# Two gate vectors summed as rows on four column groups and spread over the partitions through DRAM

## The chip, the cores and the metric

The kernel runs on one core of a Trainium2 chip. The metric is the time of the whole kernel on the device, in microseconds, the median of three runs. Beside it stands one profiled execution, whose trace is read below.

## What is computed

A trunk of two layers over 256 tokens of width 1024, all in f32. Layer 0 mixes tokens with gated linear attention (GLA), layer 1 with MoBA, a block-sparse softmax attention that has a single block of 256 keys here. Each mixer is followed by a squared-ReLU MLP of width 4096. Each of the four sub-layers is normalised and modulated (shift, scale) from a conditioning vector c, and its output is multiplied by a gate vector before it is added to x:

```python
c_act = jax.nn.silu(c)
for i in range(DEPTH):
    mod = (c_act @ ada_w[i] + ada_b[i])[:, None, :]
    sh1, sc1, g1, sh2, sc2, g2 = jnp.split(mod, 6, axis=-1)
    h = rms_norm(x, norm_mix_g[i]) * (1 + sc1) + sh1
    y = gla_mixer(h, ...) if i % 2 == 0 else moba_mixer(h, ...)
    x = x + g1 * y
    h = rms_norm(x, norm_mlp_g[i]) * (1 + sc2) + sh2
    x = x + g2 * sq_relu_mlp(h, mlp_w1[i], mlp_w2[i])
```

The four gates g1, g2 of the two layers are vectors of 1024 values. In the kernel tokens lie on the partitions, so a gate has to stand in every one of the 128 partitions.

## The kernel before

Every weight matrix goes through the same pipeline in pieces of 1 MB. SyncE's queue (SP) loads a piece into w_raw, ScalarE copies each half of it (a "unit" of 128 x 1024) to a rounded high part (L1051), and VectorE subtracts to get the low part (L1433). TensorE multiplies three times for each product, high by high, high by low and low by high (L503 to L505, L510 to L512, L698 to L700). The engines run programs written out by hand, in order, tied by counting semaphores; what stands ahead in an engine's program holds what is behind it.

The modulation c_act @ ada_w is computed beside the weights. GpSimd loads ada_w in pieces of 1 MB (load(s), L381), VectorE multiplies each by its values of c_act and accumulates over the rows that one partition has (ada(), L1450). What is left is a sum over the 128 partitions. For a shift or scale, sum_mods (L583) takes four blocks of 512 columns at once: each is multiplied by a 128 x 32 matrix of ones into its own 32 partitions of a PSUM bank. For a gate, fin_gate (L622) multiplies one block of 512 columns by 128 x 128 ones, so that the sum stands in all 128 partitions of a bank, and VectorE's gate() (L1486) adds it to the bias, which was loaded as a broadcast into the tile gates. A gate has two such blocks. The tile has room for two gates: slot 0 for a mixer's, slot 1 for an MLP's. Slots are filled again for layer 1 (gate_biases(1), L432), after SP has seen the last residual of layer 0.

The change touches these places in the order of time:
- Start: GpSimd's set-up memsets (L365, L366) ahead of its load of inv_f (L368); later, after load(5), the loads of the gate biases of layer 0 (L395).
- End of the first MLP, mlp(0) after the loop, from 326 us. TensorE: two fin_gate for the MLP's gate (blocks 10 and 11, L731), then sum_mods for the two sub-layers of layer 1. Then the last 48 products of the MLP, first the two halves of token tile 0, with the transposes of the modulation rows (L591) between them, then token tile 1. After three of the four units of tile 1 it waits for gate_ok and transposes the normalised tile 0 for MoBA (turn_norm, L631).
- VectorE there: the last split, gate() twice, two splits of MoBA's weights into the tile spare, then for each half of token tile 0 the residual, product with the gate (L1598) and addition to x (L1601), with mods() and one more split between the two. Then the norm of tile 0 (L1505 to L1509), and the low parts of its operands (L1587). ScalarE squares each half of x as it comes (L1073) and makes the operands (L1114, L1118).
- SP waits for x_new of token tile 1 of this residual, loads both gate biases of layer 1 (L432) and then goes on with MoBA's weights.
- MoBA. two_blocks runs the first two blocks of 512 columns of its input projection, and gate1() in it sums the gate of MoBA (blocks 16 and 17) after the second unit of the last group. VectorE's gate1() adds it to the bias, between two splits. turn_rot(0) (L906) transposes the first rotated tile (L1770) and waits for that gate, since both use banks 2 and 3. The gate is used by the residual at the end of MoBA.

Of the kernel before, what the change touches and what calls it, by code (L numbers as in the profile page):

```python
# [25 lines left out]
F32 = mybir.dt.float32  # L26
# [21 lines left out]
def trunk_kernel(nc, x_d, c_d, pos_d, ada_w, ada_b, mix_g, mlp_g, gla_in, gla_up, gla_bg, gla_og,  # L48
# [32 lines left out]
    with ctx:  # L81
# [17 lines left out]
        gates = sb("gates", [P, 2, D])  # L99
        eye = sb("eye", [P, P])  # L100
# [111 lines left out]
        gb_in = [sem(f"gb_in{i}") for i in range(DEPTH)]  # L212
        hi_made, lo_made = sem("hi_made"), sem("lo_made")
# [138 lines left out]
        def _(pool):  # L352
# [14 lines left out]
            pool.wait_ge(pool_set, 2)  # L367
# [6 lines left out]
            for k in range(4):  # L374
                nc.gpsimd.dma_start(glr_up[32 * k:32 * k + RANK, :], gla_up[0]).then_inc(glr_in, 16)
            def load(s):
# [12 lines left out]
            for s in range(2, 4 * N_PAIRS_ADA):  # L389
                pool.wait_ge(ada_mac, 2 * (s - 1))  # L390
                load(s)
                if s == 5:
                    nc.gpsimd.dma_start(amask[:, :], amask_d).then_inc(mask_in, 16)
                    for i in range(2):
                        nc.gpsimd.dma_start(gates[:, i], ada_b[0:1, (3 * i + 2) * D:(3 * i + 3) * D].to_broadcast([P, D])  # L395
                                            ).then_inc(gb_in[0], 16)
# [3 lines left out]
        def _(sp):  # L400
# [28 lines left out]
            def gate_biases(l):  # L429

                for s in range(2):
                    sp.dma_start(gates[:, s], ada_b[l:l + 1, (3 * s + 2) * D:(3 * s + 3) * D].to_broadcast([P, D])  # L432
                                 ).then_inc(gb_in[l], 16)
# [65 lines left out]
        def _(pe):  # L499
# [123 lines left out]

            def turn_norm(v, tb):
# [52 lines left out]
            def mlp(l):  # L677
# [52 lines left out]
                for i in range(2):  # L730
                    fin_gate(12 * l + 10 + i, i)  # L731
                if l + 1 < DEPTH:
# [18 lines left out]
                for u in range(4 if l + 1 < DEPTH else 0):  # L751
# [3 lines left out]
                    if u == 2:  # L755
                        pe.wait_ge(gate_ok, 4 * l + 4)
# [134 lines left out]
            def moba():  # L891
                def gate1():
                    pe.wait_ge(a_ok, A_NORM[2] + 8)
                    for i in range(2):
                        fin_gate(16 + i, 2 + i)

                def turn_rot(n):

                    pe.wait_ge(rot_ok, n + 1)
                    if n == 0:  # L900
                        pe.wait_ge(gate_ok, 6)
# [56 lines left out]
                two_blocks(2, mix_base[1], [in_bank(n, tb) for n in range(2) for tb in range(TB)], {1: gate1})  # L958
# [452 lines left out]
        def _(dve):  # L1411
# [69 lines left out]
            def gate(i, bank):  # L1481

                dve.wait_ge(gb_in[i // 4], 32)
                dve.wait_ge(gate_p, i + 1)
                g = gates[:, (i % 4) // 2, (i % 2) * COLS:(i % 2 + 1) * COLS]
                V.tensor_tensor(g, ps[:, bank, :], g, ALU.add).then_inc(gate_ok, 1)  # L1486

# [242 lines left out]
            def moba():  # L1730
# [43 lines left out]
                def gate1():  # L1774
                    for i in range(2):
# [240 lines left out]
```

## Time and profile before

| | us |
|---|---|
| median of 3 runs | 643.25 |
| lowest and highest | 642.64 to 643.25 |
| span of the profiled execution | 642.6 |
| TensorE busy | 617.6 |
| VectorE busy | 474.3 |
| ScalarE busy | 341.8 |
| GpSimd busy | 39.5 |

All times below are microseconds from the start of the profiled span, unless ns is written. Busy times of an engine leave out its waits and the issuing of DMAs. A line of a timeline gives start, length, engine, line of the kernel, what is written and read, and in brackets how long the engine stood idle before it and what released it. The chain is followed back from the last instruction, at each step to what released it. A time to landing runs from the issue of a DMA to its last byte and semaphore.

### The profile page before, as it was taken

What the parts mean: (1) busy time and instruction counts of PE and PEld (TensorE: products, weight loads), DVE (VectorE), ACT (ScalarE), POOL (GpSimd) and SP (SyncE); (2) the same over time, 40 slices, a digit from 0 to 9 for tenths busy, and PEclk for the clock granted to TensorE, in tenths of its full rate; (3) what the DMA queues carried; (4) which work ended last, traced back from release to release, by engine and by line L of the source; (5) the groups of instructions that cost most, each with busy time, mean ns of one, the idle gap of its engine ahead of it and who ended that gap; (6) DMA issues with size and microseconds to landing.
All of it is one profiled execution on the core that took longest, in us unless ns stands there. A gap on an engine that the chain in (4) does not pass through costs nothing.

```text
span 642.6 us, 9093 instructions
## 1 busy us (share of the span) xinstructions
PE 617.6 (96%) x3391; PEld 515.0 (80%) x3391; DVE 474.3 (74%) x660; ACT 341.8 (53%) x581; POOL 39.5 (6%) x65
## 2 busy tenths in 40 slices
PE   3699999999999999999999999999999999999997
PEld 2367875677889989998977788788789899899985
DVE  4638998898778978889897898766786555455455
ACT  3437632658654354445458688666954453444440
POOL 3030011000000101010100000000000000000000
PEclk9699999999999999999999999999999999999999
DMA  8999599678488998999982665344476555556501
GB/s 287 387 356 395 180 318 384 224 247 277 156 284 316 376 366 306 351 363 337 360 320 82 246 197 196 133 126 155 132 267 225 171 182 188 191 196 196 196 0 65
DMA packets 59084, 156.43 MB, mean 243 GB/s; under 512 B 2818, under 2 KB 3312, under 8 KB 59056
## 3 DMA queue, kind: packets, MB, share of 16 engines
q1 hardware_dynamic: 47296, 112.41, 49.9%
q0 software_dynamic: 11760, 43.67, 19.2%
q8 instruction: 15, 0.25, 0.2%
q14 instruction: 13, 0.11, 0.0%
HBM read 155.02 MB, written 1.05 MB: 243 GB/s over the span
## 4 chain that ended last, share of the span: by engine, by line
PE 82%; DVE 10%; DMA 3%; issue 2%; ACT 2%; SPq 0%; DVEq 0%; ACTq 0%
PE ps L503 14%; PE ps L504 14%; PE ps L505 14%; PE ps L700 7%; PE ps L699 7%; PE ps L698 7%; PE ps L510 4%; PE ps L511 3%; PE ps L512 3%; DMA arena<-in_ada_w_dram 3%; DVE w_lo L1433 1%; DVE spare L1433 1%; DVE ada_acc L1450 1%; PE ps L607 1%; PE ps L622 1%
## 5 line engine op out<-in xcount | busy, mean ns | idle before, releaser
L1051 ACT ACTIVATE w_hi<-w_raw 128x1024 fp32r<-128x1024 f32 x180 | 189.2, 1058 | 205.0 <-PE ps L505 107.0
L1433 DVE TENSOR_TENSOR w_lo<-w_raw,w_hi 128x1024 fp32r<-128x1024 f32 x180 | 217.9, 1222 | 94.5 <-ACT w_hi L1051 94.3
L699 PE MATMUL ps<-a_lo,w_hi 128*128 128x256 f32 x384 | 108.7, 283 | 0.0
L700 PE MATMUL ps<-a_hi,w_lo 128*128 128x256 f32 x384 | 108.7, 283 | 0.0
L698 PE MATMUL ps<-a_hi,w_hi 128*128 128x256 f32 x384 | 108.6, 283 | 0.0
L503 PE MATMUL ps<-w_hi,m_hi 128*128 128x512 f32 x256 | 100.4, 392 | 0.0
L504 PE MATMUL ps<-w_lo,m_hi 128*128 128x512 f32 x256 | 99.8, 390 | 0.0
L505 PE MATMUL ps<-w_hi,m_lo 128*128 128x512 f32 x256 | 99.7, 389 | 0.0
L503 PE MATMUL ps<-w_hi,a_hi 128*128 128x512 f32 x224 | 92.7, 414 | 5.1 <-DVE a_lo L1587 5.1
L504 PE MATMUL ps<-w_lo,a_hi 128*128 128x512 f32 x224 | 88.3, 394 | 0.0
L505 PE MATMUL ps<-w_hi,a_lo 128*128 128x512 f32 x224 | 88.3, 394 | 0.0
L1450 DVE SCALAR_TENSOR_TENSOR ada_acc<-ada_raw,c_act,ada_acc 128x1024 f32<-128x1024 f32 x56 | 71.8, 1281 | 3.6 <-DMA ada_raw<-in_ada_w_dram 2.0
L698 PEld LDWEIGHTS ps<-a_hi,w_hi 128*128 128x128 f32 x384 | 73.7, 192 | 0.5
L699 PEld LDWEIGHTS ps<-a_lo,w_hi 128*128 128x128 f32 x384 | 73.7, 192 | 0.5
L700 PEld LDWEIGHTS ps<-a_hi,w_lo 128*128 128x128 f32 x384 | 73.7, 192 | 0.0
L503 PEld LDWEIGHTS ps<-w_hi,a_hi 128*128 128x128 f32 x224 | 42.6, 190 | 19.2 <-issue 7.4
L503 PEld LDWEIGHTS ps<-w_hi,m_hi 128*128 128x128 f32 x256 | 48.1, 188 | 11.3 <-DVE w_lo L1433 0.8
L505 PEld LDWEIGHTS ps<-w_hi,m_lo 128*128 128x128 f32 x256 | 48.1, 188 | 10.1
L504 PEld LDWEIGHTS ps<-w_lo,m_hi 128*128 128x128 f32 x256 | 48.1, 188 | 9.4
L381 POOL DMA_DIRECT2D ada_raw<-in_ada_w_dram x40 | 28.2, 706 | 406.4 <-DVE ada_acc L1450 361.3
L505 PEld LDWEIGHTS ps<-w_hi,a_lo 128*128 128x128 f32 x224 | 42.6, 190 | 9.3
L504 PEld LDWEIGHTS ps<-w_lo,a_hi 128*128 128x128 f32 x224 | 42.7, 191 | 8.0
(202 smaller groups left out, 708.9 us busy)
## 6 DMA issues: line engine op xcount, KB each, us to landing
w_raw<-in_mlp_w_dram SPq DMA_DIRECT2D x64, 1024.0 KB, 5.5
ada_raw<-in_ada_w_dram POOLq DMA_DIRECT2D x40, 1024.0 KB, 6.7
w_raw<-in_gla_w_in_dram SPq DMA_DIRECT2D x12, 1024.0 KB, 14.7
w_raw<-in_moba_w_in_dram SPq DMA_DIRECT2D x12, 1024.0 KB, 7.3
ada_raw<-in_ada_w_dram SPq DMA_DIRECT2D x4, 1024.0 KB, 13.2
arena<-in_ada_w_dram SPq DMA_DIRECT2D x4, 1024.0 KB, 14.3
w_raw<-in_gla_w_out_dram SPq DMA_DIRECT2D x4, 1024.0 KB, 9.3
w_raw<-in_moba_w_out_dram SPq DMA_DIRECT2D x4, 1024.0 KB, 5.0
```

Source lines behind the costliest of these rows:

```text
L381: nc.gpsimd.dma_start(ada_pair(s), src.rearrange("(k p) n -> p k n", p=P)).then_inc(ada_sw_in[s % 2], 16)
L503: mm(out, hi, w_hi[:, slot, wc], start=first, stop=False)
L504: mm(out, hi, w_lo[:, slot, wc], start=False, stop=False)
L505: return mm(out, lo, w_hi[:, slot, wc], start=False, stop=last)
L510: mm(out, hi, unit_hi(u)[:, wc], start=first, stop=False)
L511: mm(out, hi, unit_lo(u)[:, wc], start=False, stop=False)
L698: mm(o, w_hi[:, u, w], a_hi[:, a, :], start=u == 0 and k == 0, stop=False)
L699: mm(o, w_hi[:, u, w], a_lo[:, a, :], start=False, stop=False)
L700: z = mm(o, w_lo[:, u, w], a_hi[:, a, :], start=False, stop=u == 3 and k == 1)
L1051: A(dst, w_raw[:, c // 2, c % 2], ACT.Copy).then_inc(hi_made, 1)
L1433: V.tensor_tensor(out, w_raw[:, c // 2, c % 2], w.bitcast(F32), ALU.subtract).then_inc(lo_made, 1)
L1450: z = V.scalar_tensor_tensor(acc, w, c, acc, op0=ALU.mult, op1=ALU.add)
```

## The change

The gate of the first MLP (blocks 10, 11) and that of MoBA (blocks 16, 17) are summed together at the end of the first MLP. Four products with 128 x 32 ones put them as rows into partitions 0, 32, 64 and 96 (and their neighbours) of one bank. VectorE adds the biases, which GpSimd loaded into four rows of a new tile gate_row, in one instruction. GpSimd, once it has issued load(37), waits for that, stores the four rows to a DRAM tensor of 2 x 1024, waits until they are all there, and loads each gate from it as a broadcast into its slot of gates, the MLP's first. VectorE waits for the MLP's broadcast before the first residual of the seam, and for the other before the residual of MoBA. Both fin_gate and both gate() inside MoBA are gone, as are those of the first MLP; the first gate (GLA's) and the last (the second MLP's) stay as they were. SP loads only one bias for layer 1. TensorE's waits for the old gates become a wait for gate_row_ok at the seam and for the operands in MoBA.

```diff
+        gate_row = sb("gate_row", [97, COLS])
+        gate_d = nc.dram_tensor("gate_rows", [2, D], F32).ap()
...
-            pool.wait_ge(pool_set, 2)
+            nc.gpsimd.memset(gate_row[:, :], 0.0).then_inc(pool_set, 1)
+            pool.wait_ge(pool_set, 3)
...
+            def bias_row(at, l, part):
+
+                for i in range(2):
+                    c0 = part * D + i * COLS
+                    nc.gpsimd.dma_start(gate_row[32 * (at + i):32 * (at + i) + 1, :], ada_b[l:l + 1, c0:c0 + COLS]
+                                        ).then_inc(bias_row_in, 16)
...
-                    for i in range(2):
-                        nc.gpsimd.dma_start(gates[:, i], ada_b[0:1, (3 * i + 2) * D:(3 * i + 3) * D].to_broadcast([P, D])
-                                            ).then_inc(gb_in[0], 16)
+                    nc.gpsimd.dma_start(gates[:, 0], ada_b[0:1, 2 * D:3 * D].to_broadcast([P, D])).then_inc(gb_in[0], 16)
+                    bias_row(0, 0, 5)
+                    bias_row(2, 1, 2)
+                if s == 37:
+                    pool.wait_ge(gate_row_ok, 1)
+                    for j in range(4):
+                        nc.gpsimd.dma_start(gate_d[j // 2:j // 2 + 1, (j % 2) * COLS:(j % 2 + 1) * COLS],
+                                            gate_row[32 * j:32 * j + 1, :]).then_inc(row_out, 16)
+                    pool.wait_ge(row_out, 64)
+                    for r in range(2):
+                        nc.gpsimd.dma_start(gates[:, 1 - r], gate_d[r:r + 1, :].to_broadcast([P, D])
+                                            ).then_inc(gate_in[1 - r], 16)
...
-                for s in range(2):
-                    sp.dma_start(gates[:, s], ada_b[l:l + 1, (3 * s + 2) * D:(3 * s + 3) * D].to_broadcast([P, D])
-                                 ).then_inc(gb_in[l], 16)
+                sp.dma_start(gates[:, 1], ada_b[l:l + 1, 5 * D:6 * D].to_broadcast([P, D])).then_inc(gb_in[l], 16)
...
+            def sum_gates(blocks, bank):
+
+                pe.wait_ge(ada_mac, 8 * (ada_turn(blocks[-1]) + 1))
+                for i, b in enumerate(blocks):
+                    z = mm(ps[32 * i:32 * i + 32, bank, :], ones[:, 0:32], ada_acc[:, acc_slot(b)],
+                           start=True, stop=True)
+                z.then_inc(row_p, 1)
...
-                for i in range(2):
-                    fin_gate(12 * l + 10 + i, i)
-                if l + 1 < DEPTH:
+                if l + 1 == DEPTH:
+                    for i in range(2):
+                        fin_gate(22 + i, i)
+                else:
+                    sum_gates((10, 11, 16, 17), 0)
...
-                        pe.wait_ge(gate_ok, 4 * l + 4)
+                        pe.wait_ge(gate_row_ok, 1)
...
-                        pe.wait_ge(gate_ok, 6)
+                        pe.wait_ge(a_ok, A_NORM[2] + 8)
...
+            def gate_rows(bank):
+
+                dve.wait_ge(bias_row_in, 64)
+                dve.wait_ge(row_p, 1)
+                V.tensor_tensor(gate_row[:, :], ps[0:97, bank, :], gate_row[:, :], ALU.add).then_inc(gate_row_ok, 1)
...
                 spare_units(3, range(2))
+                dve.wait_ge(gate_in[0], 16)
...
-                for i in range(2):
-                    gate(4 * l + 2 + i, i)
                 if l + 1 < DEPTH:
+                    gate_rows(0)
                     spare_units(2, range(2))
-                dve.wait_ge(gate_ok, 4 * l + 4)
+                    dve.wait_ge(gate_in[1], 16)
+                else:
+                    for i in range(2):
+                        gate(2 + i, i)
+                    dve.wait_ge(gate_ok, 4)
```

## Rows read from the trace of the kernel before

**Rows 1.** The page: busy times; the chain that ended last.

```profile
PE 617.6 (96%) x3391; PEld 515.0 (80%) x3391; DVE 474.3 (74%) x660; ACT 341.8 (53%) x581; POOL 39.5 (6%) x65
...
PE 82%; DVE 10%; DMA 3%; issue 2%; ACT 2%; SPq 0%; DVEq 0%; ACTq 0%
```

**Rows 2.** Chain in order of time, gate and modulation sums: start, length, what.

```profile
326.67 1.72 PE ps L622 x4
328.38 1.90 PE ps L583 x16
...
362.27 1.72 PE ps L622 x4
```

**Rows 3.** Timeline, TensorE, seam: start, length, instruction, [idle before, releaser].

```profile
341.51 1.06 PE L631 MATMUL ps<-eye,arena 128*128 128x128 f32 x8 [0.62 <-DVE arena L1509]
```

**Rows 4.** Timeline of VectorE, end of the first MLP and entry into MoBA.

```profile
321.06 2.60 DVE L1450 SCALAR_TENSOR_TENSOR arena<-ada_raw,c_act,arena 128x1024 f32<-128x1024 f32 x2
...
329.99 1.29 DVE L1486 TENSOR_TENSOR gates<-ps,gates 128x512 f32<-128x512 f32 x2
...
334.16 0.69 DVE L1598 TENSOR_TENSOR arena<-ps,gates 128x512 f32<-128x512 f32 x1
...
340.56 0.81 DVE L1509 TENSOR_SCALAR arena<-x,stat 128x1024 f32<-128x1024 f32 x1
```

**Rows 5.** Timeline of VectorE in MoBA's first two blocks.

```profile
366.57 1.28 DVE L1486 TENSOR_TENSOR gates<-ps,gates 128x512 f32<-128x512 f32 x2
...
369.92 1.23 DVE L1770 TENSOR_TENSOR arena<-arena,stat 128x1024 f32<-128x1024 f32 x1
```

**Rows 6.** Timeline of TensorE in MoBA: the first rotated transposes.

```profile
372.04 1.03 PE L906 MATMUL ps<-eye,arena 128*128 128x128 f32 x8
```

**Rows 7.** Timeline of GpSimd.

```profile
3.48 1.95 POOL L354 DMA_DIRECT2D rows<-in_ada_b_dram  x4
...
5.67 0.55 POOL L366 MEMSET glr_up<- 128x512 f32 x1
...
88.90 0.71 POOL L381 DMA_DIRECT2D ada_raw<-in_ada_w_dram  x1 [3.16 <-DVE ada_acc L1450]
...
323.96 0.70 POOL L381 DMA_DIRECT2D ada_raw<-in_ada_w_dram  x1 [4.08 <-DVE arena L1450]
```

**Rows 8.** DMA issues: out, in, queue, count, KB, us to landing.

```profile
x<-in_x_dram SPq DMA_DIRECT2D x2, 512.0 KB, 4.1
gates<-in_ada_b_dram POOLq DMA_DIRECT2D x2, 512.0 KB, 9.5
gates<-in_ada_b_dram SPq DMA_DIRECT2D x2, 512.0 KB, 4.7
out_dram<-x SPq DMA_DIRECT2D x4, 256.0 KB, 2.0
...
glr_up<-in_gla_w_gate_up_dram POOLq DMA_DIRECT2D x4, 32.0 KB, 6.1
...
pos_i<-in_positions_dram POOLq DMA_DIRECT2D x1, 1.0 KB, 2.0
```

**Rows 9.** Windows: length, busy of each engine (instructions), PEclk, DMA share, GB/s.

```profile
330.20:334.16 3.96, 3.96 (x26) 3.37 (x23) 3.35 (x4) 3.85 (x5) 0.00 (x0) 1.00 1.01 391
334.16:341.50 7.34, 6.73 (x30) 5.25 (x29) 5.85 (x15) 4.28 (x10) 0.00 (x0) 1.00 0.21 79
```

**Rows 10.** Windows of the start-up, same columns.

```profile
16.00:20.00 4.00, 2.57 (x21) 1.36 (x17) 3.07 (x10) 0.60 (x1) 0.00 (x0) 0.95 1.05 388
...
24.00:28.00 4.00, 1.08 (x6) 0.99 (x5) 2.81 (x6) 2.72 (x5) 0.00 (x0) 0.50 1.04 387
```

**Rows 11.** The chain in the start-up: start, length, what.

```profile
32.57 0.43 PE ps L503
...
33.39 0.23 PE ps L505
```

**Rows 12.** Timeline of VectorE in the start-up.

```profile
25.12 0.16 DVE L1459 TENSOR_TENSOR modc<-ps,cols 128x4 f32<-128x4 f32 x1 [4.84 <-PE ps L615]
```

More of the change, by code:

```diff
@@ L212, in trunk_kernel @@
         gb_in = [sem(f"gb_in{i}") for i in range(DEPTH)]
+        bias_row_in, row_p, gate_row_ok, row_out = sem("bias_row_in"), sem("row_p"), sem("gate_row_ok"), sem("row_out")
+        gate_in = [sem(f"gate_in{i}") for i in range(2)]
         hi_made, lo_made = sem("hi_made"), sem("lo_made")
@@ L891, in moba @@
             def moba():
-                def gate1():
-                    pe.wait_ge(a_ok, A_NORM[2] + 8)
-                    for i in range(2):
-                        fin_gate(16 + i, 2 + i)
                 def turn_rot(n):
@@ L957, in moba @@
                 pe.wait_ge(x_new, x_done(2, 0, 1))
-                two_blocks(2, mix_base[1], [in_bank(n, tb) for n in range(2) for tb in range(TB)], {1: gate1})
+                two_blocks(2, mix_base[1], [in_bank(n, tb) for n in range(2) for tb in range(TB)], {})
                 for n in range(2, 6):
@@ L1481, in gate @@
             def gate(i, bank):
-                dve.wait_ge(gb_in[i // 4], 32)
+                dve.wait_ge(gb_in[i // 2], 16)
                 dve.wait_ge(gate_p, i + 1)
-                g = gates[:, (i % 4) // 2, (i % 2) * COLS:(i % 2 + 1) * COLS]
+                g = gates[:, i // 2, (i % 2) * COLS:(i % 2 + 1) * COLS]
                 V.tensor_tensor(g, ps[:, bank, :], g, ALU.add).then_inc(gate_ok, 1)
+            def gate_rows(bank):
+                dve.wait_ge(bias_row_in, 64)
+                dve.wait_ge(row_p, 1)
+                V.tensor_tensor(gate_row[:, :], ps[0:97, bank, :], gate_row[:, :], ALU.add).then_inc(gate_row_ok, 1)
             def newton(r, v, b, r0):
@@ L1772, in scale @@
                                     r[:, :, None].to_broadcast([P, 8, HD]), ALU.mult).then_inc(rot_ok, 1)
-                def gate1():
-                    for i in range(2):
-                        gate(4 + i, 2 + i)
                 def top(h):
@@ L1805, in follow @@
                         rotate(0)
-                    if (n, u) == (1, 0):
-                        gate1()
                     if 1 <= n < 4:
@@ L1898, in mlp @@
                         hidden(NJ - 1, base + 8 * NJ - 4)
-                for i in range(2):
-                    gate(4 * l + 2 + i, i)
                 if l + 1 < DEPTH:
+                    gate_rows(0)
                     spare_units(2, range(2))
-                dve.wait_ge(gate_ok, 4 * l + 4)
+                    dve.wait_ge(gate_in[1], 16)
[3 more added lines that the diff above has]
+                    dve.wait_ge(gate_ok, 4)
                 for half in range(2):
```

## Prediction

> **What bounds the kernel now.** I read the page's busy shares and its chain first. TensorE is busy 96% of the span, and the chain that ended last is 82% TensorE [rows 1]. So TensorE work taken away is worth its full time wherever TensorE doesn't stop to wait, and every new stop is lost in full. The change touches two places of that engine's queue: the end of the first MLP with the entry into the MoBA layer (I call it the seam, 326 to 350 us), and the inside of MoBA's first two projection blocks (362 us). I then read the timelines of TensorE and VectorE over both, because there one wait has to be followed from engine to engine.
>
> At the seam TensorE runs two full gate sums from 326.67, 1.72 us on the chain, then two modulation sums of eight matmuls each [rows 2]. It goes straight on with the last 48 products of the MLP and stops only once, for 0.62 us until 341.51: the transposes of the next norm wait for VectorE's normalised tile (L1509) [rows 3, 4]. VectorE's queue to that tile is: gate additions at 329.99, two splits of weights, first residual at 334.16, then the modulation vectors, a split and the second residual, norm at 340.56 [rows 4]. From residual to the end of the norm that is 341.37 - 334.16 = 7.2 us. VectorE doesn't wait for TensorE anywhere in it, so this queue of VectorE, with ScalarE's squares in between, sets when TensorE goes on. Cover at the seam is therefore short: a first residual that comes later by d makes TensorE late by the whole of d, because the stop exists already.
>
> **What the change takes away.** At the end of the first MLP two full sums (1.72 us on the chain) become one group of four column-group sums. A modulation sum has that form, 16 steps of them take 1.90 us on the chain, thus 0.95 us for a group [rows 2]. TensorE saves 1.72 - 0.95 = 0.8 us there, but that only makes it arrive earlier at the stop at 341.51. I cost it at nothing; if the new wait below did not exist it would still be worth at most nothing to 0.6 us, since VectorE's queue is what is late. VectorE saves one addition of 0.64 us, hidden in the same way by the new wait.
>
> In MoBA both full gate sums go, 1.72 us on the chain [rows 2], in a stretch where TensorE never stops. The 1.28 us of additions on VectorE go too [rows 5]. What could be late next there is VectorE's rotated tile L1770, done at 369.92 + 1.23 = 371.15, for the transposes at 372.04 [rows 5, 6]. TensorE would come to them at 370.3; VectorE, 1.28 us lighter, is ready at 369.9. So the full 1.7 us is gained, and I see no wait that takes it back. Bounds: 1.3 us if VectorE's lightening is all that passes, 1.8 us at most.
>
> **What it adds: a round trip.** The summed rows must be added to the biases, stored to DRAM by GpSimd, waited for, and read back as two broadcasts; the first residual of the seam now waits for the broadcast of the MLP gate. Step by step:
> - The addition stands where the old ones stood, behind the last weight split on VectorE. It starts at 329.99 and takes half of the pair's 1.29 us, to 330.65 [rows 4]. That TensorE delivers earlier doesn't help.
> - GpSimd sees a semaphore of VectorE 0.30 us after the instruction's end (multiply-adds 321.06 + 2.60 = 323.66, load at 323.96 [rows 4, 7]). At 323.96 it issued the last weight load before this point and then it only waits, so nothing is in front. First store at 330.95.
> - Four stores are issued in a row. A small one costs the queue 1.95 / 4 = 0.49 us [rows 7]; the fourth starts at 330.95 + 3 x 0.49 = 332.4.
> - Landing of a store of 2 KB from GpSimd to DRAM isn't in the trace. The nearest rows: the 1 KB load by GpSimd and the stores of the output, both 2.0 us, before and after the full load of the DMA; 32 KB loads by GpSimd at a time of full DMA 6.1 [rows 8]. Here the DMA engines are full (share 1.01) until 334 and then empty out (mean share 0.21 to 341.5) [rows 9]. I take 4.0, the middle of 2.0 and 6.1: 336.4. It could be no lower than 2.0, as that is the floor of every row.
> - GpSimd wakes, 0.30: 336.7. The broadcast of 512 KB: 4.7 us by SP's queue for a pair, 4.1 for a plain 512 KB load, 9.5 by GpSimd's queue at a full time [rows 8]. The engines are empty by then, so I take 4.7: 341.4.
> - First residual at 341.45 instead of 334.16: 7.3 us late. All of VectorE's and ScalarE's queue behind it (both residuals, modulation vectors, norm, the operands of MoBA's first block) is late by as much, and TensorE with it. TensorE reaches its stop 0.8 us earlier, at 340.1, and would stand until 348.8: about 8.7 us. Two other queues stand behind this: SP's wait for x_new holds MoBA's next weight loads, late by as much and no more, and behind GpSimd's new waits are only the last two modulation loads, which the second MLP asks for over 100 us later.
>
> As to a rule for these two transfers: the Trainium skill (DMA: Bandwidth & Descriptors, Anatomy of one DMA) gives a GpSimd transfer 2.0 us plus bytes / 436e3 us. By it the store takes 2.0 and the broadcast 3.2 us, an estimate by that page, and the residual would start at 337.9, 3.8 us late; the sum would be 645.3 without and 647.6 with the clock term below. The trace's own 512 KB row of 4.1 us is already above the page's 3.2.
>
> **The clock after the stop.** In the start-up TensorE worked 2.57 of the 4 us from 16 to 20 and the mean granted clock was 0.95 there: it fell just before 20. From 24 to 28, with 1.08 us of work, it was 0.50 (1.2 GHz instead of 2.4) [rows 10]. The dense work that began at 28.39 ran at 0.43 us a product until 33.0, after which it was 0.23 [rows 11]. That is 11 products with 0.20 us extra each, 2.2 us. A stop of 8.7 us is longer than all idleness in either of those two stretches, so I take it that the clock falls here and costs 2.2 us. Bounds: 0 and 2.5.
>
> The Trainium skill (TensorE: Matmul & The Clock Gate, Part 1) states that an idle array goes to 1.2 GHz and needs sustained work to get back. By that rule the fall here is certain; the rows show only the fall after half-idle work.
>
> **Other edits.** The memset of the row tile (as L366's, 0.55 us) moves GpSimd's load of inv_f by as much, and VectorE's angles with it. But VectorE later waits 4.84 us for TensorE's columns, up to 25.12 [rows 12], which covers 0.55; uncovered it would cost 0.55. Four small bias loads replace one broadcast by GpSimd near 85 us: four issues of 0.49 are 2.0 us, less the one removed, in front of an idle of 3.16 us [rows 7]. SP issues one gate load less behind its wait for x_new, so the weight loads after it can only come sooner. All three at nothing.
>
> **Sum.** Profiled span 642.6; the median 643.25 is 0.65 above it, and I add the differences to the median. +7.3 (late residual) + 2.2 (clock) - 1.7 (MoBA's gate sums) = +7.8: 651.0 us.
>
> **Rivals.**
> - *The clock doesn't fall.* For it: it was at 1.00 for nearly all of 16 to 20 us with TensorE idle a third of the time [rows 10]. +7.3 - 1.7 = +5.6: 648.8. With the short landings (2.0 and 4.1) the residual starts at 338.8, 4.7 late, and the time is 646.2.
> - *The transfers are slow.* For it: the trace's two broadcasts by GpSimd's queue took 9.5 us [rows 8], and this is that form. Landings 6.1 and 9.5 put the residual at 348.3, 14.1 late: +14.6 with the clock: 657.9. Against it: those rows come from a time of full DMA.
> - *The round trip is covered, and the kernel is faster.* VectorE still has two splits to do before the residual, so the trip has from 330.65 to 334.16 for nothing, and breaks even with MoBA's gain up to 335.9. If it is all covered the time is 643.25 - 1.7 = 641.5. It needs both transfers and five issues in 5.2 us; the floor rows (2.0 and 4.1, with issues of 1.5 and wakes of 0.6) already add to 8.2. Only if the time to landing of these forms is far under any row can it be.
> - *The change doesn't do what it says:* the four sums run one after another instead of side by side. Then the seam loses nothing either, as TensorE is early at the stop; the time stays at 651.0.
>
> **How the numbers follow.** Forecast (clock falls, landings between 2.0 + 4.1 and 6.1 + 4.7): 0.58, 648.4 to 653.1. Clock stays: 0.22, 646.2 to 650.9. Slow transfers: 0.12, to 657.9. Covered: 0.05. Something between covered and the shortest landings: 0.03. Range 646.2 to 655.5: it leaves out the covered cases and the upper half of the slow one, some 0.15. This kernel's times can be told apart to about 0.2% (1.3 us): faster 0.05, same 0.02, slower 0.93.
>
> **What would show it.** VectorE idle before the first residual of the seam, released by the broadcast, some 8 us. TensorE idle before L631's transposes at about 341 us grown from 0.62 to 6 to 10 us. Granted clock 0.5 for some us behind it, with products of 0.43. No gate sum between 345 and 372 us (shifted), and the distance from MoBA's first product to its first rotated transposes shorter by 1.7 us. The forecast falls if the broadcast lands before 336, or if TensorE's stop is as short as now.

## The result and the profile after

The changed kernel takes 650.38 us (median of 4, 649.97 to 651.26) against 642.94 us before; the ratio is 1.0112, 95% interval 1.0096 to 1.0128. It is slower by 7.4 us, where 7.8 had been forecast.

| | before | after |
|---|---|---|
| median, us | 642.94 | 650.38 |
| span of the profiled execution | 642.6 | 648.4 |
| TensorE busy | 617.6 | 615.4 |
| VectorE busy | 474.3 | 472.4 |
| GpSimd busy | 39.5 | 44.8 |

The page of after, its busy times and its chain, beside [rows 1]:

```profile
PE 615.4 (95%) x3391; PEld 514.4 (79%) x3391; DVE 472.4 (73%) x657; ACT 341.6 (53%) x581; POOL 44.8 (7%) x75
...
PE 77%; DVE 12%; DMA 5%; issue 3%; ACT 2%; SPq 0%; POOL 0%; DVEq 0%; ACTq 0%
```

TensorE is busy 2.2 us less and the kernel is longer: the shares of VectorE, the DMA and issue in the chain have grown, that of TensorE has shrunk. The timeline of VectorE at the seam, which answers to [rows 4]:

```profile
328.00 0.68 DVE L1516 TENSOR_TENSOR gate_row<-ps,gate_row 97x512 f32<-97x512 f32 x1
328.82 2.36 DVE L1457 TENSOR_TENSOR spare<-w_raw,spare 128x1024 fp32r<-128x1024 f32 x2
340.20 0.69 DVE L1628 TENSOR_TENSOR arena<-ps,gates 128x512 f32<-128x512 f32 x1 [9.02 <-DMA gates<-gate_rows]
...
346.58 0.81 DVE L1539 TENSOR_SCALAR arena<-x,stat 128x1024 f32<-128x1024 f32 x1
```

Then GpSimd over the same time, and TensorE at the four sums, the transposes, the first product of MoBA and the first rotated transposes (beside [rows 3] and [rows 6]):

```profile
328.98 1.97 POOL L412 DMA_DIRECT2D gate_rows<-gate_row  x4 [6.32 <-DVE gate_row L1516]
336.13 1.07 POOL L416 DMA_DIRECT2D gates<-gate_rows  x2 [5.18 <-DMA gate_rows<-gate_row]
```

```profile
324.39 1.06 PE L647 MATMUL ps<-ada_acc,ones 128*32 128x512 f32 x8
...
347.54 1.94 PE L658 MATMUL ps<-eye,arena 128*128 128x128 f32 x8 [9.70 <-DVE arena L1539]
...
351.52 0.39 PE L529 MATMUL ps<-spare,a_hi 128*128 128x512 f32 x1
...
377.77 1.03 PE L930 MATMUL ps<-eye,arena 128*128 128x128 f32 x8
```

**How to compare the two traces.** The seam comes 2.0 us earlier in the profiled execution of after (addition at 328.00 against 329.99), before anything of the change but its start-up edits has happened. Those edits change nothing that the times show (experiment 2), so I put the 2.0 us down to scatter of single executions and take distances from that addition. In microseconds:
- addition to first residual: 4.17 before, 12.20 after: 8.0 late;
- first residual to the transposes: 341.51 - 334.16 = 7.35 before, 347.54 - 340.20 = 7.34 after: nothing is made up;
- transposes to MoBA's first product: 344.10 - 341.51 = 2.59 before, 351.52 - 347.54 = 3.98 after: 1.4 more;
- MoBA's first product to the rotated transposes: 372.04 - 344.10 = 27.94 before, 377.77 - 351.52 = 26.25 after: 1.7 less.

The sum is 8.0 + 1.4 - 1.7 = +7.7. From the addition to the end of the span it is 642.6 - 329.99 = 312.6 before and 648.4 - 328.00 = 320.4 after, +7.8: nothing else happens behind the seam.

The windows of TensorE's clock in after, of 1 us each (length, busy time of PE, PEld, DVE, ACT, POOL, then PEclk, DMA share, GB/s):

```profile
340.00:341.00 1.00, 0.00 (x0) 0.00 (x0) 0.77 (x2) 0.00 (x0) 0.00 (x0) 0.95 0.64 262
341.00:342.00 1.00, 0.00 (x0) 0.00 (x0) 0.95 (x4) 0.35 (x1) 0.00 (x0) 0.50 0.00 0
...
350.00:351.00 1.00, 1.00 (x4) 0.71 (x4) 0.42 (x1) 0.97 (x3) 0.00 (x0) 0.50 0.00 0
351.00:352.00 1.00, 1.00 (x6) 0.82 (x5) 0.27 (x1) 0.97 (x4) 0.00 (x0) 0.93 0.00 0
```

TensorE's products end at 337.8; the granted clock falls to 0.50 (1.2 GHz) just before 341 and is back just after 351.0, 3.5 us after the transposes began. It was low for ten microseconds, but for six and a half of them TensorE had nothing to do. How much of the low stretch falls on work differs between executions, as the table behind experiment 8 shows.

### The profile page after: what moved, and what is told of

The parts are those of the page before. It is cut to its first block, busy times and chain, and to the rows that moved or that the text cites. A ratio compares the mean times of both kernels' runs of the same rounds, so it can differ in the third digit from the quotient of the medians.

```text
span 648.4 us, 9096 instructions
## 1 busy us (share of the span) xinstructions
PE 615.4 (95%) x3391; PEld 514.4 (79%) x3391; DVE 472.4 (73%) x657; ACT 341.6 (53%) x581; POOL 44.8 (7%) x75
## 3 DMA queue, kind: packets, MB, share of 16 engines
HBM read 155.02 MB, written 1.06 MB: 241 GB/s over the span
## 4 chain that ended last, share of the span: by engine, by line
PE 77%; DVE 12%; DMA 5%; issue 3%; ACT 2%; SPq 0%; POOL 0%; DVEq 0%; ACTq 0%
PE ps L522 13%; PE ps L523 13%; PE ps L524 13%; PE ps L727 7%; PE ps L726 7%; PE ps L725 7%; PE ps L529 4%; PE ps L531 3%; PE ps L530 3%; DMA arena<-in_ada_w_dram 2%; DVE w_lo L1457 2%; DMA ada_raw<-in_ada_w_dram 2%; DVE spare L1457 1%; DVE arena L1474 1%; DVE ada_acc L1474 1%
## 6 DMA issues: line engine op xcount, KB each, us to landing
ada_raw<-in_ada_w_dram SPq DMA_DIRECT2D x4, 1024.0 KB, 12.9
```

## Experiments

**1. Nobody waits for the trip.** The stores and broadcasts stay, but slot 1 of the gates is filled early with the biases alone. So this kernel leaves out the summed part of the first MLP's gate and its output is not the reference's.

```diff
+                    nc.gpsimd.dma_start(gates[:, 1], ada_b[0:1, 5 * D:6 * D].to_broadcast([P, D])).then_inc(gate_in[1], 16)
                     bias_row(0, 0, 5)
...
-                    for r in range(2):
-                        nc.gpsimd.dma_start(gates[:, 1 - r], gate_d[r:r + 1, :].to_broadcast([P, D])
-                                            ).then_inc(gate_in[1 - r], 16)
+                    nc.gpsimd.dma_start(gates[:, 0], gate_d[0:1, :].to_broadcast([P, D])).then_inc(cut_in, 16)
+                    pool.wait_ge(cut_in, 16)
+                    nc.gpsimd.dma_start(gates[:, 0], gate_d[1:2, :].to_broadcast([P, D])).then_inc(gate_in[0], 16)
```

> The changed kernel with the round trip left in place but nobody waiting for it: the broadcast of the first MLP's gate row goes to slot 0 and is overwritten by MoBA's, and slot 1 holds the biases alone, loaded at 85 us. So the first MLP's output is multiplied by its gate's bias and not by the whole gate. Theory A (the loss is VectorE's wait for the broadcast, 8.0 us, and 1.4 us of slow TensorE clock behind it; MoBA's two gate sums give 1.7 us back): 641.2 us, TensorE's stop at the seam back at under 1 us, clock 1.00 there. Rival B (the stores, the broadcasts and GpSimd's issues cost by themselves, by contention or as time outside the span): 645 or more.

Measured: 640.88 us against 643.16 before, ratio 0.9957 (0.9937 to 0.9977). VectorE at the seam, then TensorE at the transposes:

```profile
327.66 0.68 DVE L1518 TENSOR_TENSOR gate_row<-ps,gate_row 97x512 f32<-97x512 f32 x1
328.89 2.36 DVE L1459 TENSOR_TENSOR spare<-w_raw,spare 128x1024 fp32r<-128x1024 f32 x2 [0.55 <-ACT spare L1077]
331.17 0.68 DVE L1630 TENSOR_TENSOR arena<-ps,gates 128x512 f32<-128x512 f32 x1
```

```profile
338.51 1.06 PE L660 MATMUL ps<-eye,arena 128*128 128x128 f32 x8 [0.59 <-DVE arena L1541]
```

With the same sums, stores and GpSimd work, the whole loss is gone once the wait is gone. Rival B is refuted. The gain is 2.3 us by the medians (1.5 to 4.1 by the interval), where MoBA's sums account for 1.7. In the traces the other 0.6 lies at the seam: from the addition to the residual it is 3.51 us here and 4.17 before (4.37 in experiment 2, which has the old sums too). The split on VectorE waits for ScalarE's copy (0.55 in the row above; 0.60 before), ScalarE's copies stand behind its reading of the modulation rows, and these behind TensorE's sums. So most of TensorE's saving gets through to VectorE, where nothing else holds it; that VectorE itself has one addition less is needed for it too.

**2. The start-up edits alone**, on the kernel before: tile, memset, and the four loads of bias rows.

```diff
+            nc.gpsimd.memset(gate_row[:, :], 0.0).then_inc(pool_set, 1)
+            pool.wait_ge(pool_set, 3)
...
+                            nc.gpsimd.dma_start(gate_row[32 * (at + i):32 * (at + i) + 1, :], ada_b[l:l + 1, c0:c0 + COLS]
+                                                ).then_inc(bias_row_in, 16)
```

> The kernel before with the start-up edits alone: the row tile, its memset, and four loads of bias rows (used by nobody), both broadcasts kept. In the trace of the changed kernel everything from the first matmuls of the start-up on is about 2 us earlier than before, while the time outside its span is about 1.2 us longer. Theory A: neither belongs to the change; 642.9 us within 0.6. Rival B: the edits move the start-up by 1 to 2 us either way, 641 or 644.5.

Measured: 643.05 against 643.16 us, ratio 0.9996 (0.9983 to 1.0009). Nothing clear of the noise, as theory A has it. The first weight product of the start-up, first in after, then in this kernel:

```profile
27.49 0.77 PE L522 MATMUL ps<-w_hi,a_hi 128*128 128x512 f32 x1 [3.30 <-DVE a_lo L1617]
```

```profile
25.38 0.76 PE L511 MATMUL ps<-w_hi,a_hi 128*128 128x512 f32 x1 [3.31 <-DVE a_lo L1595]
```

It stood at 28.39 before, 3.0 us later than in this kernel with an equal median. Among traces with this same start-up code it stands between 25.38 and 28.08 (experiment 4). It doesn't carry over to the seam as it is: the gate additions come at 328.89 here against 329.99 before, 1.1 us apart and not 3.0. So neither number says much about a change. The times of the kernel before, measured beside experiments 5 to 8, lie between 642.15 and 645.61, and in each of those executions the time is 1.7 us or more above the span. So the profiled execution of before, with its span of 642.6, was one of the slower of its kind.

**3. TensorE kept busy in its stop** with 36 spare products.

```diff
+                        for _ in range(WARM):
+                            mm(ps[:, 0, :], m_hi[:, 3, tile(1)], w_hi[:, 3, 0:COLS], start=True, stop=True)
                         pe.wait_ge(mod_red, 4 + v + 2)
                         turn_norm(v + 1, 0)
```

> The changed kernel with 36 spare products of 128 x 512 (each 0.23 us, 8.3 us in all) put into the 9.7 us in which TensorE stands before the next norm's transposes. Their result is not used. Theory A (the granted clock falls in the stop and costs 1.4 us after it): the clock stays 1.00, transposes take 1.06 us instead of 1.94, time 649.0. Rival B (the slow clock is covered by ScalarE and VectorE, which are what is late): clock 1.00 but time 650.4 as without.

Measured: 649.39 us, ratio 1.0101 (1.0077 to 1.0125): 6.2 us above before, against 7.4. TensorE, then two windows:

```profile
338.46 8.32 PE L788 MATMUL ps<-w_hi,m_hi 128*128 128x512 f32 x36
347.84 1.06 PE L659 MATMUL ps<-eye,arena 128*128 128x128 f32 x8 [1.05 <-DVE arena L1542]
...
350.43 0.47 PE L530 MATMUL ps<-spare,a_hi 128*128 128x512 f32 x1
```

```profile
346.00:348.00 2.00, 0.95 (x6) 0.52 (x5) 1.49 (x4) 1.97 (x4) 0.00 (x0) 1.00 0.00 0
348.00:350.00 2.00, 2.00 (x14) 1.68 (x13) 0.97 (x2) 1.62 (x5) 0.00 (x0) 1.00 0.00 0
```

The clock stays at 1.00 and transposes to MoBA's first product takes 350.43 - 347.84 = 2.59 us, to the hundredth what it took before. The clock's part is 1.4 us in this pair of traces. The times give 0.7 (by the ratios) to 1.2, with an interval (1.0077 to 1.0125) that overlaps that of after, so they alone show no gain. The table behind experiment 8 has more traces for it.

**4. The row sum earlier.** The same sum behind the first unit of down projection j = 5, with the last two turns of TensorE's loop written out, VectorE's addition after its multiply-adds of unit c = 4, the stores behind modulation load 33 and the broadcasts behind load 34.

```diff
-                with pe.Fori(1, NJ - 1) as j:
+                with pe.Fori(1, NJ - 3 if l == 0 else NJ - 1) as j:
...
+                    def rows_now():
+                        pe.wait_ge(relu_ok, 2 * (m0 + NJ - 2) + 2)
+                        sum_gates((10, 11, 16, 17), 0)
...
+                        if l == 0 and c == 4 and isinstance(j, int) and j == NJ - 3:
+                            gate_rows(0)
```

> The changed kernel with the same four-row sum one and a half blocks of the MLP earlier, behind the first unit of the down projection j = 5 (about 296 us), and the trip behind modulation loads 33 and 34. Nothing waits for it at the seam. Theory A: the residual starts when VectorE comes to it; the seam has 1.72 us less on TensorE, 0.9 us of row sums are paid in the loop, MoBA gives 1.7 us: 640.4 us, faster than both. Rival B (the trip is slow because the DMA is full, and it slows the weights that the loop needs, or the early sum makes TensorE wait for VectorE): 642 or more.

Measured: 643.13 us, ratio 0.9995 (0.9983 to 1.0007). The seam's wait is gone and so is the gain. GpSimd, then VectorE:

```profile
308.96 1.06 POOL L417 DMA_DIRECT2D gates<-gate_rows  x2 [1.38 <-DMA gate_rows<-gate_row]
310.48 0.71 POOL L393 DMA_DIRECT2D ada_raw<-in_ada_w_dram  x1 [0.47 <-DVE arena L1485]
```

```profile
323.48 2.60 DVE L1485 SCALAR_TENSOR_TENSOR arena<-ada_raw,c_act,arena 128x1024 f32<-128x1024 f32 x2 [3.79 <-DMA ada_raw<-in_ada_w_dram]
```

The multiply-adds at 323.48 need load 35, issued at 310.48 behind 1 MB of broadcasts in the same queue. It landed 12.9 us later; the median of these loads is 6.5 to 7.6 us, by the trace. Theory A missed what the broadcasts are in front of.

**5. The same with the broadcasts out of the way**: the MLP's behind load 35, MoBA's behind load 37.

```diff
-                if s == 34:
+                if s == 35:
                     pool.wait_ge(row_out, 64)
-                    for r in range(2):
-                        nc.gpsimd.dma_start(gates[:, 1 - r], gate_d[r:r + 1, :].to_broadcast([P, D])
-                                            ).then_inc(gate_in[1 - r], 16)
+                    nc.gpsimd.dma_start(gates[:, 1], gate_d[0:1, :].to_broadcast([P, D])).then_inc(gate_in[1], 16)
+                if s == 37:
+                    nc.gpsimd.dma_start(gates[:, 0], gate_d[1:2, :].to_broadcast([P, D])).then_inc(gate_in[0], 16)
```

> As e_early, but the broadcast of the MLP's gate is issued behind modulation load 35 instead of in front of it, and MoBA's behind load 37 at the seam. In e_early VectorE stood 3.79 us at 319.7 us for load 35, which was behind 1 MB of broadcasts in GpSimd's queue and took 12.9 us to land. Theory A (that stall was the whole of what was missing): it goes, and the time is 643.1 - 3.8 + 1.2 for what of it the seam would have absorbed, 640.5 us, or 0.9963 of before. Rival B (the early row sum costs the loop its time by itself, through VectorE being 97% busy there): 642 to 643.

Measured: 640.29 us against 643.20 before, ratio 0.9949 (0.9929 to 0.9968). It beats both kernels. GpSimd, VectorE and TensorE:

```profile
309.05 0.71 POOL L393 DMA_DIRECT2D ada_raw<-in_ada_w_dram  x1 [2.92 <-DVE arena L1485]
309.76 0.55 POOL L416 DMA_DIRECT2D gates<-gate_rows  x1
```

```profile
331.68 0.68 DVE L1639 TENSOR_TENSOR arena<-ps,gates 128x512 f32<-128x512 f32 x1
```

```profile
339.01 1.06 PE L659 MATMUL ps<-eye,arena 128*128 128x128 f32 x8 [0.57 <-DVE arena L1550]
```

The first residual waits for nothing. Rival B is refuted: what was missing in experiment 4 was the stall of 3.79 us, of which the times get back 2.8. That the row sums cost the loop no more than the seam is as far as the times tell: experiment 1, with the sums at the seam, has 0.9957 (0.9937 to 0.9977).

**6. The trip again at a quiet time**, by the same queue, behind the first.

```diff
+                    pool.wait_ge(gate_in[0], 16)
+                    pool.wait_ge(gate_in[1], 16)
+                    for j in range(4):
+                        nc.gpsimd.dma_start(gate_e[j // 2:j // 2 + 1, (j % 2) * COLS:(j % 2 + 1) * COLS],
+                                            gate_row[32 * j:32 * j + 1, :]).then_inc(row_out, 16)
+                    pool.wait_ge(row_out, 128)
+                    nc.gpsimd.dma_start(gates[:, 0], gate_e[1:2, :].to_broadcast([P, D])
+                                        ).then_inc(gate_in[0], 16)
```

> The changed kernel with a second trip right behind the first, by the same queue, from 341 us on, when the DMA engines are empty: four stores to another DRAM tensor and one broadcast of 512 KB of MoBA's gate. Theory A (full engines make the store slow): the second stores land in 2.0 to 2.5 us against 5.0 for the first, the broadcast in about 4 us as in the first trip. Rival C (GpSimd's way or the DRAM target makes it slow): 5 us again. The time is that of the changed kernel, 650.4, as nobody waits for the second trip.

Measured: 650.8 us in its one run. The DMA issues of this kernel (out, in, queue, count, KB, median us to landing):

```profile
gates<-gate_rows POOLq DMA_DIRECT2D x2, 512.0 KB, 4.6
...
gates<-gate_rows_again POOLq DMA_DIRECT2D x1, 512.0 KB, 3.7
...
gate_rows_again<-gate_row POOLq DMA_DIRECT2D x4, 2.0 KB, 1.5
```

and the chain of the same kernel over the first trip:

```profile
330.49 5.40 DMA gate_rows<-gate_row
```

The same store by the same queue takes 1.5 us when the DMA engines are idle and 5.4, from the last issue, when SP's weight loads are under way. So neither GpSimd's queue nor the DRAM target makes it slow by itself, and rival C is refuted in that form. The trip pays the difference, 3.9 us, for coming behind SP's loads.

What the store waits for can be read from the packets. The DMA of after from 332.5 to 335.5, SP's queue (q1) and GpSimd's (q0): packets, MB, share.

```profile
q1 hardware_dynamic: 294, 0.57, 49.1%
q0 software_dynamic: 128, 0.01, 2.9%
```

The four rows are 128 small packets here (the second trip above has 128 too). None of the rows' packets is sent before 332.5, 2 us after the last issue, and the last 4 of them go between 335.0 and 335.5 together with the last 2 of SP's. GpSimd goes on at 336.13. It is the same in every trace of a trip at the seam by this queue (last issue before the wait; the half microsecond with the last packets of SP's queue; GpSimd's next issue):

| trace | last issue | SP's last packets | GpSimd goes on |
|---|---|---|---|
| after | 330.46 | 335.0 to 335.5 | 336.13 |
| changed kernel, second trace | 330.35 | 334.5 to 335.0 | 335.40 |
| experiment 1 | 330.1 | 333.5 to 334.0 | 334.90 |
| experiment 3 | 330.84 | 335.0 to 335.5 | 336.31 |
| experiment 6 | 330.49 | 335.0 to 335.5 | 336.17 |
| experiment 8, first trace | 331.91 | 336.5 to 337.0 | 337.63 |
| experiment 8, second trace | 329.61 | 334.5 to 335.0 | 335.47 |

GpSimd goes on 0.4 to 0.9 us after SP's last half microsecond, and 4.8 to 5.9 us after the last issue. So in all seven the landing goes with the end of SP's loads and not with the issue; the time from issue to landing is what is left between the two. Why the last row packets go no earlier, with a DMA share of only 0.26 from 334.0, 0.06 from 334.5 and 0.02 from 335.0 in after, isn't shown.

**7. The trip by ScalarE's queue.** ScalarE issues the stores, does its four copies, waits for the stores and issues the broadcasts.

```diff
+                    act.wait_ge(gate_row_ok, 1)
+                    for j in range(4):
+                        nc.scalar.dma_start(gate_d[j // 2:j // 2 + 1, (j % 2) * COLS:(j % 2 + 1) * COLS],
+                                            gate_row[32 * j:32 * j + 1, :]).then_inc(row_out, 16)
                     spare_units(2)
+                    act.wait_ge(row_out, 64)
+                    for r in range(2):
+                        nc.scalar.dma_start(gates[:, 1 - r], gate_d[r:r + 1, :].to_broadcast([P, D])
+                                            ).then_inc(gate_in[1 - r], 16)
```

> The changed kernel with the four stores and two broadcasts issued by ScalarE's queue instead of GpSimd's: ScalarE waits for the row, issues the stores, copies four units of MoBA's weights (3.9 us), waits for the stores and issues the broadcasts. Theory A (the 5 us of a store are DMA engines full with SP's weights, whoever issues): about the same landings, the trip within 1 us of the 12.2 us of the changed kernel, time 649.5 to 651. Rival C (they belong to GpSimd's way of issuing): landings of 2 us as for the output's stores, the trip 3 us shorter, time 647.

Measured: 648.73 us, ratio 1.0088 (1.0062 to 1.0113). ScalarE, then VectorE (whose addition stands at 327.06 here):

```profile
327.78 1.35 ACTq L1408 DMA_DIRECT2D gate_rows<-gate_row  x4
329.23 3.90 ACT L1066 ACTIVATE spare<-w_raw 128x1024 fp32r<-128x1024 f32 x4 [1.91 <-issue]
333.08 0.83 ACTq L1413 DMA_DIRECT2D gates<-gate_rows  x2
```

```profile
337.03 0.69 DVE L1627 TENSOR_TENSOR arena<-ps,gates 128x512 f32<-128x512 f32 x1 [4.34 <-DMA gates<-gate_rows]
```

The trip is 337.03 - 327.06 = 10.0 us, 2.2 shorter than the 12.2 of after: more than theory A allowed and less than rival C asked. The first store goes out at once and not 0.30 us later and four issues take 1.35 instead of 1.97, together 0.6 us up to the last issue. The other 1.5 us lie between the last store's issue and the broadcast's: ScalarE comes back at 333.08, 4.2 us after its last issue at 328.9, and the rows have landed. The broadcast is 0.1 shorter. The packets show that the rows were there before ScalarE came. First from 330.5 to 333.0, then from 334.0 to 334.5 (q10 is ScalarE's queue; its later packets are the broadcasts'):

```profile
q1 hardware_dynamic: 333, 0.65, 71.9%
q10 hardware_dynamic: 8, 0.01, 0.9%
...
q10 hardware_dynamic: 21, 0.09, 68.1%
q1 hardware_dynamic: 3, 0.00, 2.2%
```

The four rows are 8 packets in this queue and not 128. All have gone by 332.5 (none is left between 332.5 and 334.0), 3.6 us after the last issue, while SP's queue still has packets behind 334.0. So theory A fails in "whoever issues": beside SP's loads the stores of this queue didn't wait for the drain in this trace, where GpSimd's did in all seven. That the number of packets is the reason isn't shown. By the times the gain of 1.7 us is likely but not beyond doubt: the intervals of this kernel and of after overlap (1.0113 and 1.0096), and this trace is of an execution of 646.78 us, 2.0 under the kernel's median.

**8. Two stores instead of four before the wait.**

```diff
-                    for j in range(4):
...
-                    pool.wait_ge(row_out, 64)
                     for r in range(2):
+                        for i in range(2):
+                            j = 2 * r + i
+                            nc.gpsimd.dma_start(gate_d[r:r + 1, i * COLS:(i + 1) * COLS],
+                                                gate_row[32 * j:32 * j + 1, :]).then_inc(row_out, 16)
+                        pool.wait_ge(row_out, 32 * (r + 1))
```

> The changed kernel with only the MLP gate's two rows stored before the wait; its broadcast goes out, then MoBA's two rows and broadcast follow. Theory A (a store lands a fixed time, 5 us, after its issue, so two issues of 0.49 us fewer shorten the trip by 1.0 us, and each us of the trip is a us of the kernel): 649.4 us, VectorE's wait 8.0 instead of 9.0. Rival B (stores land only when SP's weight loads have drained at about 335 us, however early they are issued): 650.3.

Measured: 651.50 us, ratio 1.0128 (1.0101 to 1.0154), although the trip in its trace was 1.1 us shorter (330.42 to 341.48). So it was measured once more, beside the changed kernel itself.

> The changed kernel as it is, once more, as the measure for the next one on the same chip: 1.0112 of before, 650.4 us. In its second profile the trip from the row's addition to the first residual should again take 12.2 us; executions differ by 1 to 2 us in the start-up and in the loads of the first MLP, ahead of the seam, so the distance from the row's addition to the end of the span is the better measure: 320.4 us again.

> The kernel of e_pair once more, since its time (651.5) and its trace disagreed: the trip had become 1.1 us shorter (11.1 against 12.2), but the seam came 2.4 us later in that execution, 1.9 of it from the first MLP's loads, where this kernel has no edit. Theory A (the trip's 1.1 us are gained, the rest was scatter ahead of the seam): 1.0 us under e_after of the same call, and 319.4 to 319.7 us from the row's addition to the end. Rival D (something of the edit costs it back behind the seam, MoBA's later stores and broadcast): the same time as e_after or more, and a distance of 320.4 or more.

Measured: the changed kernel 651.26 us, ratio 1.0116 (1.0093 to 1.0140); two stores first 649.97 us, ratio 1.0093 (1.0074 to 1.0111). GpSimd and VectorE of the changed kernel in its second trace:

```profile
328.87 1.96 POOL L412 DMA_DIRECT2D gate_rows<-gate_row  x4 [6.37 <-DVE gate_row L1516]
335.40 1.06 POOL L416 DMA_DIRECT2D gates<-gate_rows  x2 [4.57 <-DMA gate_rows<-gate_row]
```

```profile
339.60 0.69 DVE L1628 TENSOR_TENSOR arena<-ps,gates 128x512 f32<-128x512 f32 x1 [8.12 <-DMA gates<-gate_rows]
```

and of the kernel with two stores first:

```profile
329.10 1.02 POOL L414 DMA_DIRECT2D gate_rows<-gate_row  x2 [6.50 <-DVE gate_row L1517]
335.47 0.54 POOL L417 DMA_DIRECT2D gates<-gate_rows  x1 [5.36 <-DMA gate_rows<-gate_row]
```

```profile
339.44 0.69 DVE L1629 TENSOR_TENSOR arena<-ps,gates 128x512 f32<-128x512 f32 x1 [7.73 <-DMA gates<-gate_rows]
```

The trip was 12.2 and 11.7 us with four stores, 11.1 and 11.3 with two. But the saved issues are not the reason. The last row store was issued earlier (329.61 against 330.35 in the second traces) and its landing came no earlier: GpSimd goes on at 335.47 and 335.40, both times when SP's queue has drained (table in experiment 6). So for the store the rival B of the first expectation holds (stores land when SP's weight loads have drained), and theory A's fixed time after the issue is refuted: it is 5.4 and 5.6 us with two stores against 4.8 and 5.4 with four. What is shorter is the broadcast, which now goes out alone: from its issue to the residual 3.85 and 3.97 us against 4.07 and 4.20. The rest of the differences in the trip is when the loads drain: over the seven traces GpSimd goes on 7.2 to 8.2 us after the addition.

The times don't resolve any of this. The ratios were 1.0128 against 1.0112 of after at first, and 1.0093 against 1.0116 for the second pair, with intervals that overlap both times. From the addition to the end of the span, where 319.4 to 319.7 had been expected, it is 319.7 in the first trace and 648.5 - 328.1 = 320.4 in the second, against 648.4 - 327.9 = 320.5 for the changed kernel's second. Where the second trace loses what its shorter trip gained is seen in the table below: its low clock cost more.

**All traces side by side** (row sum added, first residual, span, and from the residual to the end of the span):

| trace | addition | residual | span | residual to end | clock at the transposes |
|---|---|---|---|---|---|
| before | 329.99 | 334.16 | 642.6 | 308.4 | 1.00 |
| experiment 1 | 327.66 | 331.17 | 637.9 | 306.7 | 1.00 |
| experiment 3 | 328.38 | 340.50 | 647.2 | 306.7 | 1.00 |
| experiment 4 | in the loop | 334.83 | 641.5 | 306.7 | 1.00 |
| experiment 5 | in the loop | 331.68 | 638.4 | 306.7 | 1.00 |
| after | 328.00 | 340.20 | 648.4 | 308.2 | 0.50 |
| changed kernel, second trace | 327.89 | 339.60 | 648.4 | 308.8 | 0.50 |
| experiment 6 | 328.02 | 340.46 | 649.0 | 308.5 | 0.50 |
| experiment 7 | 327.06 | 337.03 | 645.0 | 308.0 | 0.50 |
| experiment 8, first trace | 330.42 | 341.48 | 650.1 | 308.6 | 0.50 |
| experiment 8, second trace | 328.12 | 339.44 | 648.5 | 309.1 | 0.50 |

Wherever the clock stays, the kernels with the new sums have 306.7 us behind the residual, 1.7 less than before: that is MoBA's part. Wherever it falls they have 308.0 to 309.1, so the low clock costs 1.3 to 2.4 us, and the 1.4 to 1.5 of after is near the low end.

## Why the prediction was right, point by point

The mechanism held at each step. That the sum came within 0.4 us is in part luck: against the trace of after, the lateness was forecast 0.7 too short and the clock 0.8 too dear, and within the lateness the store was 1.4 too short and the broadcast 0.7 too long.

- **The late residual: 7.3 forecast, 8.0 measured.** The mechanism held step by step: the addition in its old place, a wake of GpSimd of 0.30 us, issues of 0.49, the wait, the broadcast. The store was mis-sized: 4.0 was taken, the middle between quiet and full, and it took 5.4 from the last issue. The 2.0 that the prediction called the floor of every row was not one either: a quiet store took 1.5. The prediction looked for a landing time, where the rows wait for SP's loads to drain (experiment 6). The trace before had that moment, but rows 9 hide it in a mean share of 0.21 up to 341.5. In before, in half microseconds (DMA share next to last):

```profile
336.50:337.00 0.50, 0.50 (x4) 0.42 (x3) 0.50 (x1) 0.16 (x1) 0.00 (x0) 1.00 0.09 33
337.00:337.50 0.50, 0.50 (x4) 0.42 (x3) 0.50 (x2) 0.00 (x0) 0.00 (x0) 1.00 0.00 0
```

SP's loads are over about 337.0 there, 7.0 us behind the addition. With them as the bound GpSimd would go on at 337.4 or later and not at 336.7. The broadcast, at a quiet time, took 4.0 where 4.7 was taken. In the other traces of kernels with this wait and GpSimd's four stores the residual is 7.5 to 8.3 us late, not always 8.0.
- **The Trainium skill's figure for the store.** The 2.0 us that the Trainium skill gives as the fixed cost of a GpSimd transfer (DMA: Bandwidth & Descriptors, Anatomy of one DMA) is close to the 1.5 us of the quiet store. Here it was 5.4 behind SP's loads, which the sentence doesn't cover. The Trainium skill (DMA: Bandwidth & Descriptors, Latency and other measured facts) has the memory's own latency grow tenfold at high load, from 0.2 to 2 us. That can't be what is long here: the rows' last packets go after 335.0, 4.5 us after the last issue, and GpSimd goes on 1.1 us later at most.
- **TensorE's wait equals VectorE's lateness.** Right: the stretch from residual to transposes is 7.35 and 7.34 us. The stop itself was forecast at 8.7 and was 9.7, since the trip was longer.
- **The clock: 2.2 forecast, 1.4 measured in after, 1.3 to 2.4 over six traces.** It fell, as forecast, and the start-up's rows had the right kind of event. In after the low clock lasted 3.5 us after work resumed and not the 4.6 of the start-up (28.39 to 33.0), and the first part of it is the eight transposes, 1.94 us instead of 1.06, behind which TensorE used to wait 0.15 us for VectorE anyway. The other traces show that this length differs from execution to execution, so 2.2 lies inside what single executions show. Experiment 3 confirms the term in its trace. The rival in which the clock stays is refuted for this stop: it fell in all six traces in which TensorE stood for 7.1 to 9.7 us.
- **MoBA's gate sums: 1.7 forecast, 1.7 measured** (27.94 to 26.25 us).
- **TensorE's earlier arrival at the seam**, costed at nothing: it was worth nothing in the changed kernel, where the new wait swallows it. But the reason given, that VectorE's queue alone is late, was incomplete: without the wait 0.66 us come through, by way of ScalarE (traces of experiment 1), just above the bound of 0.6.
- **The other edits at nothing:** right for those of the start-up, to within the interval of experiment 2. SP's one load less was not taken apart.
- **The rival "one after another"** is refuted: the four sums start at 324.39 and what follows at 325.27, so they take 0.88 us, where 0.95 was taken for a group side by side.
- **The rival of slow transfers** has the broadcast wrong: at the quiet time of the seam it took 4.0. Its 9.5 is what a broadcast takes in a full stretch (9.9 in experiment 5).
- **The span and the median.** The prediction took a median 0.65 us above the profiled span. That compares two executions; within one of after the time is 1.8 us above the span (650.17 and 648.4). As only differences were added to the median, nothing followed from it.
- **The covered rival** failed as the prediction argued against it: the trip needs 12.2 us and has about 4.

## What to carry to other kernels

A hop through DRAM in place of arithmetic is priced by its two landings, its issues and what is in the DMA queues at that moment, and it is free only if it starts that much ahead of its first reader; here that meant moving the sum one and a half loop turns up, which turned +1.1% into -0.5%. For a small store behind bulk loads, read from the trace when those loads drain before you look for a landing time: here that moment set the landing, and issuing the store earlier gained nothing. When a trip is moved into a busy stretch, look at what its bulk transfers are in front of in their own queue, not only at who waits for them. And before summing single instructions, look whether the engine that gets longer stops would fall into a lower clock: here its slow restart cost 1.3 to 2.4 us, a fifth of the loss in after.

## What the runs showed of the hardware

- A store of 2 KB to DRAM from GpSimd's queue landed in 1.5 us with idle DMA engines. Behind SP's weight loads it landed 4.5 to 5.6 us after the last issue, and in all seven traces within a microsecond of the last packets of those loads. From ScalarE's queue four such rows were 8 packets instead of 128, and were through 3.6 us after the last issue, ahead of SP's last packets (one trace).
- A broadcast of 512 KB from GpSimd's queue landed in 3.7 to 4.6 us at a quiet time and in 9.9 in the full one of experiment 5. Two of them in front of a 1 MB load in the same queue made that load land in 12.9 us.
- In after, TensorE was idle from 337.8, kept its full clock until just before 341 and had it again 3.5 us after work resumed. Over six traces with such a stop the low clock cost 1.3 to 2.4 us; 36 spare products in the stop kept the clock, with 1.05 us of idleness left.
- Traces with the same start-up code have their first weight product between 25.38 and 28.08 us, and the row sum's addition, where it stands at the seam, comes between 327.06 and 330.42. So a comparison of two single traces needs a common point behind the scatter.
